# A diffusion backbone layer on one core: the ConvFFN's features are multiplied on GpSimd and stored as one array

## The reference

```python
h2 = _rmsnorm(x, g_pre_ffn) * (1 + sc2) + sh2
up = _dwconv_rows(jnp.einsum('bld,df->blf', h2, w_up), conv_w, conv_b, grid)   # 3 taps along a row
ug, uv = jnp.split(up, 2, axis=-1)
f = jnp.einsum('blf,fd->bld', jax.nn.gelu(ug) * uv, w_down)
x = x + gt2 * _rmsnorm(f, g_post_ffn)
```

## Time and profile before

| what | value |
|---|---|
| median of 3 runs | 1790.45 us (1790.24 to 1790.88) |
| profiled execution, its own time | 1790.83 us |
| its span in the trace | 1789.0 us |
| PE busy | 1770.3 us (99%) |
| DVE, ACT, POOL busy | 1121.8, 682.6, 213.2 us |
| granted clock of PE | 0.999 of full |
| moved by DMA | 248.55 MB, mean 139 GB/s |

### The profile page before, as it was taken

One profiled execution on the slowest core, in us unless ns is written; L12 is line 12 of the kernel. 1 busy time (PEld: TensorE's weight loads), 2 busy tenths in 40 slices (PEclk: granted clock), 3 DMA queues, 4 the chain that ended last, 5 costly groups with the idle time before them and its releaser, 6 DMA issues.

```text
span 1789.0 us, 26885 instructions
## 1 busy us (share of the span) xinstructions
PE 1770.3 (99%) x10627; PEld 1658.7 (93%) x10627; DVE 1121.8 (63%) x2396; ACT 682.6 (38%) x1132; POOL 213.2 (12%) x234
## 2 busy tenths in 40 slices
PE   8999999999999999999999999999999999999997
PEld 3999999999999999999988999999999999888886
DVE  4786566566566544463555688777777777666664
ACT  3723212333144243451344544444444444343432
POOL 1010000100000100010010252222222220020101
PEclk9999999999999999999999999999999999999999
DMA  9133334424433544373232323333333336868682
GB/s 349 50 99 113 94 102 128 123 79 149 108 115 126 147 114 146 131 250 113 96 123 87 111 96 101 101 101 101 100 101 101 101 110 207 273 223 295 226 279 89
DMA packets 213105, 248.55 MB, mean 139 GB/s; under 512 B 11216, under 2 KB 173148, under 8 KB 212980
## 3 DMA queue, kind: packets, MB, share of 16 engines
q1 hardware_dynamic: 195444, 183.54, 33.2%
q0 software_dynamic: 13056, 46.39, 7.6%
q10 hardware_dynamic: 4480, 16.91, 2.3%
HBM read 190.20 MB, written 56.59 MB: 138 GB/s over the span
## 4 chain that ended last, share of the span: by engine, by line
PE 89%; DVE 7%; ACT 1%; SPq 1%; POOL 1%; issue 1%; DMA 1%; DVEq 0%; ACTq 0%
PE ps L1265 23%; PE ps L1293 14%; PE ps L925 11%; PE ps L927 11%; PE ps L926 11%; PE ps L1207 5%; PE ps L1090 2%; PE ps L1091 2%; PE ps L1092 2%; PE ps L1074 2%; PE ps L1078 2%; PE ps L1076 2%; DVE H_lo L1894 1%; DVE T_full L595 1%; DVE ring_lo L1894 1%; DVE ada_part L2113 1%
## 5 line engine op out<-in xcount | busy, mean ns | idle before, releaser
L925 PE MATMUL ps<-H_hi,ring_hi 128*128 128x384 f32 x1224 | 422.8, 345 | 0.9 <-DVE H_lo L1894 0.3
L927 PE MATMUL ps<-H_hi,ring_lo 128*128 128x384 f32 x1224 | 409.7, 335 | 0.0
L926 PE MATMUL ps<-H_lo,ring_hi 128*128 128x384 f32 x1224 | 409.6, 335 | 0.0
L925 PEld LDWEIGHTS ps<-H_hi,ring_hi 128*128 128x128 f32 x1224 | 229.9, 188 | 4.2 <-DVE H_lo L1894 2.1
L926 PEld LDWEIGHTS ps<-H_lo,ring_hi 128*128 128x128 f32 x1224 | 230.1, 188 | 1.0
L927 PEld LDWEIGHTS ps<-H_hi,ring_lo 128*128 128x128 f32 x1224 | 229.8, 188 | 0.0
L1265 PE MATMUL ps<-T_hi,up_hi 128*128 128x288 f32 x608 | 130.3, 296 | 1.2 <-DVE up_lo L1894 1.2
L2077 DVE SCALAR_TENSOR_TENSOR Cst<-Cst,GE,ps 128x257 f32<-128x257 f32 x56 | 27.0, 482 | 165.9 <-PE ps L1078 165.9
L1894 DVE TENSOR_TENSOR down_lo<-down_raw,down_hi 128x1024 fp32r<-128x1024 f32 x66 | 80.7, 1222 | 80.3 <-ACT f_hi L1791 80.3
L1265 PE MATMUL ps<-T_lo,up_hi 128*128 128x288 f32 x608 | 130.3, 296 | 0.0
L1265 PE MATMUL ps<-T_hi,up_lo 128*128 128x288 f32 x608 | 130.2, 296 | 0.0
(11 more groups left out here) (296 smaller groups left out, 3548.0 us busy)
## 6 DMA issues: line engine op xcount, KB each, us to landing
down_raw<-in_w_down_dram SPq DMA_DIRECT2D x66, 512.0 KB, 3.9
raw<-in_w_in_dram SPq DMA_DIRECT2D x44, 512.0 KB, 4.2
up_raw<-in_w_up_dram SPq DMA_DIRECT2D x38, 512.0 KB, 5.3
raw<-in_w_ada_dram SPq DMA_DIRECT2D x32, 512.0 KB, 5.4
f_raw<-z_gate SPq DMA_DIRECT2D x66, 192.0 KB, 3.8
v_raw<-z_value SPq DMA_DIRECT2D x66, 192.0 KB, 4.2
z_gate<-mid_g SPq DMA_DIRECT2D x38, 288.0 KB, 3.6
z_value<-mid_v SPq DMA_DIRECT2D x38, 288.0 KB, 4.8
```

The lines of the kernel that those rows point to most:

```text
L925: pe.matmul(out, whi, xhi, start=first, stop=False)
L926: pe.matmul(out, whi, xlo, start=False, stop=False)
L927: return pe.matmul(out, wlo, xhi, start=False, stop=last)
```

## The change

Features are multiplied by POOL as soon as gate and value are there, in place: `plain_feature(f)` writes the product over `conv_v`, block by block, and `feature_half(s, half)` writes it over `mid["v0"]` or `mid["g1"]`. One array goes to DRAM and back, and DVE's `feature_product` is gone. What had waited for a store of the gate now waits for the product (`feature_done`). Apart from this, DVE makes `up_lo` of index 2 for s = 0 (`next_weights(-1, 2)`) ahead of the outer taps of the last value block.

```diff
             def plain_store(f):
-                sp.wait_ge(gelu_done, NB * (f + 1))
-                sp.dma_start(gate_dram[f], conv_g[:, :]).then_inc(plain_g_stored, 16)
-                sp.wait_ge(conv_value_done, NB * (f + 1))
-                sp.dma_start(value_dram[f], conv_v[:, :]).then_inc(plain_v_stored, 16)
+                sp.wait_ge(feature_done, NB * (f + 1))
+                sp.dma_start(f_dram[f], conv_v[:, :]).then_inc(plain_stored, 16)
...
-                sp.dma_start(f_raw[n % DR][:, :], gate_dram[k][:, cols]).then_inc(f_in[n % DR], 16)
-                sp.dma_start(v_raw[n % DR][:, :], value_dram[k][:, cols]).then_inc(f_in[n % DR], 16)
+                sp.dma_start(f_raw[n % DR][:, :], f_dram[k][:, r * BW:(r + 1) * BW]).then_inc(f_in[n % DR], 16)
...
-                half_store(s, "g0")
-                half_store(s, "v1")
...
+            def plain_feature(f):
+                for b in range(NB):
+                    tok = slice(b * BW, (b + 1) * BW)
+                    pool.wait_ge(gelu_done, NB * f + b + 1)
+                    pool.wait_ge(conv_value_done, NB * f + b + 1)
+                    pool.tensor_tensor(conv_v[:, tok], conv_v[:, tok], conv_g[:, tok], ALU.mult).then_inc(feature_done, 1)
+
+            def feature_half(s, half):
+
+                pool.wait_ge(up_gelu, 2 * s + half + 1)
+                pool.wait_ge(tap_done, 4 * s + (2 if half else 3))
+                out = f_half[half][:, :]
+                pool.tensor_tensor(out, mid[f"g{half}"][:, :], mid[f"v{half}"][:, :], ALU.mult).then_inc(feature_done, 1)
+
             pool.wait_ge(h_split_done, 2 * NB * KD)
             for k in range(2):
                 quarter_tiles(pool, pool_sums, k, 8 * k)
+            plain_feature(0)
+            plain_feature(1)
             for s in range(NP):
-                for j in range(4):
-                    weight_sum(s, j)
+                weight_sum(s, 0)
+                if s >= 2:
+                    feature_half(s - 2, 0)
+                weight_sum(s, 1)
+                weight_sum(s, 2)
+                if s >= 2:
+                    feature_half(s - 2, 1)
+                weight_sum(s, 3)
+                if s == 0:
+                    plain_feature(2)
+            for s in (NP - 2, NP - 1):
+                feature_half(s, 0)
+                feature_half(s, 1)
...
-                    act.wait_ge(plain_g_stored, 16 * PLAIN)
+                    act.wait_ge(feature_done, NB * PLAIN)
...
                             if f:
-                                act.wait_ge(plain_v_stored, 16 * f)
+                                act.wait_ge(plain_stored, 16 * f)
                         else:
                             act.wait_ge(done0, Q_FF + 3 * f + b + 1)
                             if f:
-                                act.wait_ge(plain_g_stored, 16 * f)
+                                act.wait_ge(feature_done, NB * (f - 1) + b + 1)
...
             def down_split(n):
 
                 d = n % DR
-                if n + 1 < NB * NF:
-                    feature_product(n + 1)
...
                 if (f, block) == (2, 4):
                     quarter_split(3)
+                    next_weights(-1, 2)
 
             plain_up(0, [[2], [3]])
             plain_up(1, [[4], [5]])
             plain_up(2, [[], []])
-            for i in range(2, 6):
+            for i in range(3, 6):
                 next_weights(-1, i)
```

More of the change, by code:

```diff
@@ L337, in build @@
     g_at = [LD0 + 8192 + 4 * T] + [HH0 + 4 * T * (4 + n) for n in range(1, DR)]
-    v_at = [LD0 + 8192 + 4 * T + 4 * BW] + [HH0 + 32 * T + 4 * T * (4 + n) for n in range(1, DR)]
     f_raw = [place(f"f_raw{n}", [P, BW], at=at) for n, at in enumerate(g_at)]
-    v_raw = [place(f"v_raw{n}", [P, BW], at=at) for n, at in enumerate(v_at)]
     x1ld = place("x1ld", [P, 4, DM], at=R)
@@ L423, in build @@
     product_done, product_held, output_summed = S("product_done"), S("product_held"), S("output_summed")
-    tap_started, tap_done, up_gelu, f_ready = S("tap_started"), S("tap_done"), S("up_gelu"), S("f_ready")
-    half_stored = {n: S(f"half_stored_{n}") for n in ("g0", "g1", "v0", "v1")}
+    tap_started, tap_done, up_gelu = S("tap_started"), S("tap_done"), S("up_gelu")
+    half_stored = [S("half_stored0"), S("half_stored1")]
     down_in, f_in = [S(f"down_in{n}") for n in range(DR)], [S(f"f_in{n}") for n in range(DR)]
@@ L681, in up_load, with half_store @@
                                  up_src(PLAIN + s, half)).then_inc(sem, 16)
[L683 to L691, removed]
+            def half_store(s, half):
+                sp.wait_ge(feature_done, NB * PLAIN + 2 * s + half + 1)
+                sp.dma_start(f_dram[PLAIN + s][:, half * HT:(half + 1) * HT], f_half[half][:, :]).then_inc(half_stored[half], 16)
             def plain_store(f):
-                sp.wait_ge(gelu_done, NB * (f + 1))
-                sp.dma_start(gate_dram[f], conv_g[:, :]).then_inc(plain_g_stored, 16)
-                sp.wait_ge(conv_value_done, NB * (f + 1))
-                sp.dma_start(value_dram[f], conv_v[:, :]).then_inc(plain_v_stored, 16)
+                sp.wait_ge(feature_done, NB * (f + 1))
+                sp.dma_start(f_dram[f], conv_v[:, :]).then_inc(plain_stored, 16)
             def down_load(n):
@@ L711, in f_load @@
                 if n == 0:
-                    sp.wait_ge(plain_v_stored, 16 * PLAIN)
+                    sp.wait_ge(plain_stored, 16 * PLAIN)
                 elif n < DR:
                     sp.wait_ge(product_done, 7 * (NP - 1) + 2)
-                if k < PLAIN:
-                    sp.wait_ge(plain_g_stored, 16 * (k + 1))
-                    sp.wait_ge(plain_v_stored, 16 * (k + 1))
+                if r == 0 and k < PLAIN:
+                    sp.wait_ge(plain_stored, 16 * (k + 1))
                 elif r == 0:
-                    for sem in half_stored.values():
-                        sp.wait_ge(sem, 16 * (k - PLAIN + 1))
-                cols = slice(r * BW, (r + 1) * BW)
-                sp.dma_start(f_raw[n % DR][:, :], gate_dram[k][:, cols]).then_inc(f_in[n % DR], 16)
-                sp.dma_start(v_raw[n % DR][:, :], value_dram[k][:, cols]).then_inc(f_in[n % DR], 16)
+                    for half in range(2):
+                        sp.wait_ge(half_stored[half], 16 * (k - PLAIN + 1))
+                sp.dma_start(f_raw[n % DR][:, :], f_dram[k][:, r * BW:(r + 1) * BW]).then_inc(f_in[n % DR], 16)
             sp.wait_ge(h_split_done, 2 * NB * KD)
@@ L743, in _ @@
                 if s:
[L744 to L745 removed]
+                    half_store(s - 1, 0)
+                    half_store(s - 1, 1)
                 if s == NP - 1:
@@ L753, in _ @@
                 f_load(n)
-            half_store(NP - 1, "v0")
-            half_store(NP - 1, "g1")
+            half_store(NP - 1, 0)
+            half_store(NP - 1, 1)
             for n in range(DR + 2, NB * NF):
```

22 lines of the change are left out of this document (8 added, 14 removed).

## The result

The changed kernel takes 1800.05 us (median of 5 runs, 1799.6 to 1801.65) against 1790.45 for the kernel before (now of 5 runs, 1790.2 to 1790.88): a ratio of 1.0054 with a 95% interval of 1.0039 to 1.0069. The profiled execution is the longest of the five, 1801.65 us, with a span of 1799.8 us. The forecast was 1800.4 us.

The account below looks back on a forecast made before the run. PE bounds the kernel from product (0, 2) on, and DVE sets that start. Product (0, 2) 9.9 us later (10.2 + 0.9 - 1.15) on 1790.83 gives 1800.7, as median 1800.4 us; range 1796.5 to 1804.5.

Parts of the forecast that it names:

- Steps 1 to 3: Plain tile 1: ACT's `conv_g` write waits for POOL's 1.03 us product behind sixteen quarter operations; DVE's taps 9.2 us late.
- Step 4: Gate blocks of plain tile 1: `T_lo` of k = 0 meets a quiet POOL, so lateness falls to 6.3 us.
- Step 5: From there to `T_lo` of k = 1: two `T_full` delays by POOL's products instead of one; late by 7.3 us.
- Step 6: `T_lo` of k = 1 runs beside a product and two weight sums: +2.9 us, late by 10.2.
- Steps 7 and 8: Tile 2 to product (0, 2): PE stands 7.3 us before product (0, 0); product (0, 2) begins 9.9 us later.
- the clock rival: PE's gaps drop the clock to 1.2 GHz; costs only if product (0, 2) runs so: +3.2, 1803.6 us; chance 0.12.
- What costs nothing: Later ACT waits, block-tile products on POOL and stores are covered; down stage between 0 and -0.5 us, taken as 0.
- signs of being wrong: PE waits in the block stage, clock below 1.00 behind 1099, `T_lo` of k = 1 near 2.75, product far from 1.03.
- POOL and DVE did not miss each other: Rival: step 6's weight sums fall on taps and cost nothing: +7.0, 1797.5 us; no collision at all 1795.6; chance 0.15.
- the first product was not done early: Rival: first product done before ACT's move at 1039.50, so nothing is late: 1788.8 us; chance 0.03.
- nothing made up for the wait: Rival of no change: DVE makes up all but 1.2 us on the way; chance 0.02.
- POOL's load in the block tiles is covered: Rival: covers of 4 to 6 us fail and 17 block tiles lose up to 1 us each: up to 1817; chance 0.04.

Follow-up runs that it names:

- e1: Changed kernel with plain tile 0's three products on POOL between the quarter operations of k = 0 and k = 1; 1797.37 us (1.0038).
- e3: Changed kernel without the moved weights, the low part back behind the last value taps; 1802.15 us (1.0063).
- e6: Changed kernel with the first quarter operation of k = 1 done two more times on POOL, making POOL 3.0 us later; 1803.91 us (1.0073).
- e5: Changed kernel with the first two weight sums of block tile 0 ahead of plain tile 1's products on POOL; 1799.61 us (1.0049).
- e2: Kernel before with the moved low part of the weights alone; 1790.08 us (0.9994).
- e4: Changed kernel with only the block tiles' products on POOL, plain tiles stored and multiplied as before, weights moved; 1790.2 us (0.9996).
- e9: Changed kernel with unread matmuls filling both PE gaps, the second gap's 24 ahead of the wait for `T_lo`; 1800.19 us (1.0054).
- e8: Changed kernel with tile 0's products between the quarter operations and two weight sums ahead of tile 1's products; 1795.88 us (1.0028).

## Why the prediction was right, point by point

The time was forecast at 1800.4 and is 1800.05. The mechanism was the one forecast, and e1, e3 and e6 take it apart with numbers. Read from DVE's rows, the 9.30 us by which product (0, 2) is late are 9.13 for the wait, -2.91 for `T_lo` of k = 0 on a quiet POOL, +0.41 for `T_full` operations, +3.02 for `T_lo` of k = 1, +0.81 for `T_lo` of k = 3 and -1.16 for the moved weights.

- *Steps 1 to 3, the wait.* Quarter operations done at 1049.0 as said; a product of 384 columns takes 0.99 us (2.96 for three) for 1.03, and 1.40 where it meets DVE (1063.47); the first one ends at about 1050.0. Taps 9.1 us late for 9.2. e6 (+2.97 for 3.0) shows that nothing covers it, e1 that the products' place in POOL's queue makes it.
- *Step 4.* Late by 6.24 us at 1058.44, forecast 6.3. `T_lo` in 2.75 us as in the row taken for it.
- *Step 5, the term that was off.* I gave each meeting of a product with a `T_full` the full +1.0 us of the earlier trace rows. They took 1.46 us (1064.03) and 1.45 (1068.15): 0.7 above the 0.76 of one alone. Two such for one of 1.0 make +0.4, not +1.0. Late by 6.65 at `T_lo` of k = 1, forecast 7.3.
- *Step 6.* 5.77 us, forecast 5.66 from the row of k = 0. By the Trainium skill's rule ("SBUF — State Buffer", section "SBUF: two separate sides") 6.4 were due, both engines' work in turn. The trace agrees that each holds up the other, but 5.77 us is nearer to the other row than to that sum: 0.6 us of the two engines' work ran side by side, and which part of it did, no run shows. e5 shows that the weight sums make the difference: one meeting left, 3.57 us. The sums and the meetings are shown; that it is the shared path and nothing else is the skill's account, which no run here tests apart.
- *Steps 7 and 8.* Product (0, 0) at 1088.47 (forecast 1089.0), product (0, 2) 9.30 us late (forecast 9.9); step 5 accounts for 0.6 of each. The distance between the two is 10.3 us, forecast 10.4, but the second gap within it is 1.86 us where I wrote 4: the clock took 1.9 us of it, as the clock rival had said it might ("comes out of the second gap"). The moved weights give 1.17 to 1.18 us (e2, e3), forecast 1.15.
- *What costs nothing.* It held: no wait of PE in the block stage, which is 1.5 us longer by the clock alone, and a down stage of 270.52 for 270.51 us. e4 shows both without the rest.
- *The clock.* I wrote that the second gap is like a stretch that kept 1.00, and gave a loss there 0.12. That comparison failed: PE stood only 1.86 us ahead of product (0, 2) in the profiled execution, and still the clock was at 1.2 GHz from 1099.4 to 1102.7. A granted clock below 1.00 behind 1099 was one of my signs of being wrong, and there it is. It cost 1.5 us, not 3.2. In the median of the five it seems to cost next to nothing: e9, whose clock stays at 1.00, has the same median to 0.14 us. The forecast of 9.95 us over the median of before stands against 9.6 measured. Part of that nearness is luck: step 5 was 0.6 too high, and the 0.3 by which 9.6 exceeds PE's 9.3 are there in e9 as well (9.59 for 9.31), so they are hardly the clock's. They lie far inside the interval, which goes from 7.0 to 12.4 us, and what they are I can't say.

The other rivals fell: POOL and DVE did not miss each other (5.77 us), the first product was not done early, nothing made up for the wait, and POOL's load in the block tiles is covered (e4). Nor are the meetings the main cost, the rival of e1: 4.6 of the 9.3 us went with no fewer meetings.

## What to carry to other kernels

- When a multiply moves to another engine, look at what stands ahead of it in that engine's queue at the moment when a buffer has to come free. The product cost 1 us; waiting for it cost 9, because sixteen operations stood in front and its output freed the buffer that ACT writes next.
- Taking work off an engine pays where that engine's lateness reaches the bound. Here DVE lost 66 multiplies in a stage in which PE waited 0.5 us in all, and the wait was added in the only stage in which DVE set PE's start.
- A queue's order can be tested cheaply: move the block by a few places (e1), or make the queue later by a known dose (e6), and compare the lateness, not only the time.

## What the runs showed of the hardware

- The granted clock fell in or behind gaps of PE much shorter than the program's end suggested, where it had kept 1.00 for some 4 us without work, and it did not fall in each. In e1 it fell behind the first gap, of 1.99 us, ahead of which PE had been busy for 42.00 of 42 us (1040 to 1082). Behind the second gap the block stage lost 1.5 us in the changed kernel (gap 1.86 us), 1.5 in e1 (2.15) and 2.2 in e8 (3.62), and nothing in e5 (1.61), e6 (1.62) and e3 (3.62; 418.89 us). The length of the gap alone does not order these. What does, the runs leave open.
- DVE and POOL can slow each other without harm to the end: in e4 DVE is busy 30 us longer in the block stage for nearly the same work, and PE not a tenth of a microsecond later. Busy time that grows is not yet time that is lost.
- A matmul pair of 288 columns takes 0.48 us at 1.2 GHz and 0.27 at 2.4 GHz.
